# An expert stage in which the second layer of each pair of experts is issued one pair behind its first layer

## The reference, cut to what matters

```python
def body(acc, blk):
    tok, wt, e = blk
    xb = h[tok]
    hid = jax.nn.silu(xb @ w1[e]) * (xb @ w3[e])
    return acc.at[tok].add(wt[:, None] * (hid @ w2[e]).astype(f32)), None
...
routed, _ = lax.scan(body, jnp.zeros(h.shape, f32), (row_tok, row_w, block_e))
shared = (jax.nn.silu(h @ sw1) * (h @ sw3)) @ sw2
return routed.astype(h.dtype) + shared
```

## Time and profile before

| | |
|---|---|
| median of 3 runs | 2049.9 us (2045.67 to 2057.2) |
| the profiled execution: its own time | 2056.09 us |
| its span in the trace | 2054.3 us |
| mean granted PE clock | 0.951 |
| first first layer of the expert stage begins (pair 0) | 1387.0 us |
| last second layer of it begins (pair 47) | 2018.7 us |

### The profile page before, as it was taken

How to read it: one execution, slowest core, us unless ns; L and a number is a source line. 1 busy time by engine, 2 the same in 40 slices (tenths; PEclk the granted TensorE clock), 3 DMA queues, 4 the chain that set the end, 5 groups by cost and what they waited for, 6 DMA issues and landing times.

```text
span 2054.3 us, 33761 instructions
## 1 busy us (share of the span) xinstructions
PE 1905.8 (93%) x14498; PEld 1387.8 (68%) x14498; DVE 973.7 (47%) x1357; ACT 651.8 (32%) x1012; POOL 238.1 (12%) x226
## 2 busy tenths in 40 slices
PE   7979998999997999899998889979899999999993
PEld 7878998999987999665756779864344444444440
DVE  5745555556564777645555664762221111111116
ACT  5544334444454333320134523231111111111110
POOL 2100000000000000012100134301111111111213
PEclk9999999999998999999898799989999999999996
DMA  8535555544444876455410000187989989989886
GB/s 274 186 107 163 186 185 185 166 133 155 144 138 145 290 247 227 144 166 171 148 41 24 12 3 4 31 324 312 387 341 376 383 343 380 381 343 379 317 353 251
DMA packets 192326, 438.68 MB, mean 214 GB/s; under 512 B 24257, under 2 KB 145601, under 8 KB 163009
## 3 DMA queue, kind: packets, MB, share of 16 engines
q1 hardware_dynamic: 156336, 352.02, 46.7%
q0 software_dynamic: 23040, 43.05, 6.2%
q10 hardware_dynamic: 12816, 41.69, 5.3%
HBM read 501.68 MB, written 26.21 MB: 257 GB/s over the span
## 4 chain that ended last, share of the span: by engine, by line
PE 85%; DVE 8%; ACT 3%; DMA 3%; issue 1%; POOL 0%; SPq 0%; ACTq 0%; DVEq 0%; POOLq 0%
PE psum L344 32%; PE psum L3371 15%; PE psum L3392 8%; PE psum L1565 7%; PE psum L3342 4%; PE psum L1572 2%; PE psum L2602 2%; DMA mem<-in_exp_w_dram 1%; ACT w_hi L400 1%; PE psum L2586 1%; DVE mem L3496 1%; DVE w_lo L405 1%; PE psum L564 1%; PE psum L3132 1%; PE psum L1087 1%
## 5 line engine op out<-in xcount | busy, mean ns | idle before, releaser
L405 DVE TENSOR_TENSOR w_lo<-mem,w_hi 128x2048 fp32r<-128x2048 f32 x122 | 279.2, 2290 | 231.0 <-ACT w_hi L400 228.4
L344 PE MATMUL psum<-x_hi,w_hi 128*128 128x256 f32 x1216 | 349.7, 288 | 4.4 <-DVE x_lo L551 4.4
L3371 PE MATMUL psum<-mem 128*64 128x512 f32 x1536 | 342.7, 599 | 9.1 <-DMA mem<-in_exp_w_dram 9.1
L344 PE MATMUL psum<-x_hi,w_lo 128*128 128x256 f32 x1216 | 344.6, 283 | 0.0
L344 PE MATMUL psum<-x_lo,w_hi 128*128 128x256 f32 x1216 | 343.7, 283 | 0.0
L400 ACT ACTIVATE w_hi<-mem 128x2048 fp32r<-128x2048 f32 x122 | 233.8, 1918 | 193.8 <-PE psum L344 190.8
L3371 PEld LDWEIGHTS psum<-mem 128*64 128x64 f32 x1536 | 110.7, 138 | 233.1 <-issue 214.7
L344 PEld LDWEIGHTS psum<-x_hi,w_hi 128*128 128x128 f32 x1216 | 234.0, 192 | 10.1 <-DVE w_lo L405 4.7
L344 PEld LDWEIGHTS psum<-x_lo,w_hi 128*128 128x128 f32 x1216 | 237.5, 195 | 0.6
L344 PEld LDWEIGHTS psum<-x_hi,w_lo 128*128 128x128 f32 x1216 | 236.5, 194 | 0.0
L3392 PE MATMUL psum<-mem 128*64 128x512 f32 x768 | 177.2, 604 | 1.0 <-DVE mem L3443 1.0
(11 more groups left out here) (500 smaller groups left out, 2959.3 us busy)
## 6 DMA issues: line engine op xcount, KB each, us to landing
mem<-in_exp_w_dram SPq DMA_DIRECT2D x192, 1024.0 KB, 12.4
mem<-in_dil_w_qkv_dram SPq DMA_DIRECT2D x36, 1024.0 KB, 5.3
mem<-in_ada_w_dram POOLq DMA_DIRECT2D x48, 512.0 KB, 4.8
y_rows<-mem ACTq DMA_DIRECT2D x48, 512.0 KB, 7.9
mem<-in_ffn_w_gate_dram SPq DMA_DIRECT2D x22, 1024.0 KB, 5.6
mem<-in_ffn_w_up_dram SPq DMA_DIRECT2D x22, 1024.0 KB, 5.6
mem<-in_ffn_w_down_dram SPq DMA_DIRECT2D x22, 1024.0 KB, 4.7
mem<-in_w_in_dram SPq DMA_DIRECT2D x13, 1024.0 KB, 5.7
```

The costliest lines, as they stand in the source:

```text
L344: ins = pe.matmul(out, lhs[a], rhs[b], start=start and k == 0, stop=stop and k == 2, **kw)
L405: dve.tensor_tensor(w_lo[n % SLOTS][:, 0, :], ring[:, n % SLOTS, :], w_hi_f[n % HI][:, 0, :], ALU.subtract).then_inc(S("w_split"), 1)
L3371: ins = pe.matmul(psum[r, up, :].rearrange("p (a n) -> p a n", a=2), xg[:, b % 2, c, x * P + 64 * e:x * P + 64 * e + 64], w_up[s][e][:, :, ...
```

## The change

The second layer of pair k - 1 moves behind the first layer and the first gather call of pair k (the new function `down`), ahead of the transposes of pair k. DVE's scaling of a result (`y_dve`) and ACT's store follow it by one pair. SP issues the second-layer loads of pair k - 1 behind the first-layer loads of pair k, and POOL does so for spare pairs. The four additions of round 0 move behind the last pair. Nothing is computed in another way.

```diff
@@ moe_sp
-        for k, (kind, n) in enumerate(PAIRS):
-            if kind != "own":
-                continue
+        for k, (kind, n) in enumerate(PAIRS + [("end", 0)]):
...
-            if k >= 2:
-                sp.wait_ge(*at("mx_up", k - 1))
-            up_rows(k, n, range(2))
-            if k >= 2:
-                sp.wait_ge(*at("mx_y", k - 1))
-            down_rows(k, n, range(2))
+            if kind == "own":
+                if k >= 2:
+                    sp.wait_ge(*at("mx_up", k - 1))
+                up_rows(k, n, range(2))
+            if k == 0:
+                down_rows(k, n, range(2))
+            elif k >= 3 and PAIRS[k - 1][0] == "own":
+                sp.wait_ge(*at("mx_y", k - 2))
+                down_rows(k - 1, PAIRS[k - 1][1], range(2))
@@ moe_pool
+            if kind == "spare":
+                fetch_up(k, n)
+            if k > 2 and PAIRS[k - 1][0] == "spare":
+                fetch_down(k - 1, PAIRS[k - 1][1])
@@ moe_pe
+        def down(k):
+            s = k % 2
+            pe.wait_ge(*at("hid_T", k + 1))
+            pe.wait_ge(*loaded(k, "down_in", 32))
+            after(pe, "y1", k)
+            for h in range(2):
+                for f in range(2):
+                    for e in range(2):
+                        r = slice(64 * e, 64 * e + 64)
+                        ins = pe.matmul(psum[r, 4 + h, :], hid_T[:, f, r], w_down[s][e][:, f, 512 * h:512 * h + 512],
+                                        start=f == 0, stop=f == 1)
+            ins.then_inc(S("mx_y"), 1)
...
             if b + 1 < BATCHES:
                 gather_pe(pe, b + 1, 2 * x)
+            if k:
+                down(k - 1)
             pe.wait_ge(*at("mx_hid", k + 1))
...
             if b + 1 < BATCHES:
                 gather_pe(pe, b + 1, 2 * x + 1)
-            pe.wait_ge(*at("hid_T", k + 1))
...
-            ins.then_inc(S("mx_y"), 1)
+        down(len(PAIRS) - 1)
@@ moe_act
-            y_out(act, k)
+            if k:
+                y_out(act, k - 1)
+        y_out(act, len(PAIRS) - 1)
@@ moe_dve
             dve.tensor_tensor(hid_tok, sil, bank((0, 6)[k % 2], 256, 256), ALU.mult).then_inc(S("mx_hid"), 1)
+            if k:
+                y_dve(dve, k - 1)
             dve.wait_ge(*at("hid_turned", k + 1))
             after(dve, "mx_y", k)
             dve.tensor_copy(hid_T, bank(1, 256).rearrange("p (c j) -> p c j", c=2)).then_inc(S("hid_T"), 1)
-            if k == 47:
-                add_taken(dve, 0, 1)
-            dve.wait_ge(*at("mx_y", k + 1))
...
-            if k == 46:
-                add_taken(dve, 0, 0)
...
-        for r in range(1, 3):
+        y_dve(dve, len(PAIRS) - 1)
+        for r in range(3):
             for t in range(NT):
                 add_taken(dve, r, t)
```

More of the change, by code:

```diff
@@ L3310, in fetch, with fetch_up @@
                                     bounds_check=EXPERTS * P - 1, oob_is_err=False).then_inc(S(done), 16)
[L3312 to L3316, removed]
+        def fetch_up(k, n):
             pool.wait_ge(*at("mx_up", k - 1))
@@ L3319, in moe_pool, with fetch_down @@
                 for m, w in enumerate(("exp_w1_2", "exp_w3_2")):
-                    fetch(w_rows[s][2 * x + m], w, 2 * n + x, "spare_up_in")
+                    fetch(w_rows[k % 2][2 * x + m], w, 2 * n + x, "spare_up_in")
+        def fetch_down(k, n):
             pool.wait_ge(*at("mx_y", k - 1))
             for x in range(2):
-                fetch(w_rows[s][4 + x], "exp_w2_2", 2 * n + x, "spare_down_in")
+                fetch(w_rows[k % 2][4 + x], "exp_w2_2", 2 * n + x, "spare_down_in")
+        pool.wait_ge(*at("spare_rows", 3))
+        for k, (kind, n) in enumerate(PAIRS):
+            if kind == "spare":
+                fetch_up(k, n)
+            if k > 2 and PAIRS[k - 1][0] == "spare":
+                fetch_down(k - 1, PAIRS[k - 1][1])
     def after(eng, name, n):
@@ L3431, in one_hot_dve, with y_dve @@
                           ).then_inc(S("one_hot"), 1)
+    def y_dve(dve, k):
+        dve.wait_ge(*at("mx_y", k + 1))
+        if k >= 2:
+            dve.wait_ge(*at(f"y_out{k % 2}", 16 * (k // 2)))
+        dve.tensor_tensor(y[:, k % 2, :], banks(4, 2), g2_b, ALU.mult).then_inc(S("y1"), 1)
     def moe_dve(dve):
@@ L3443, in moe_dve @@
             dve.tensor_copy(hid_T, bank(1, 256).rearrange("p (c j) -> p c j", c=2)).then_inc(S("hid_T"), 1)
-            if k == 47:
-                add_taken(dve, 0, 1)
-            dve.wait_ge(*at("mx_y", k + 1))
-            if k >= 2:
-                dve.wait_ge(*at(f"y_out{k % 2}", 16 * (k // 2)))
-            dve.tensor_tensor(y[:, k % 2, :], banks(4, 2), g2_b, ALU.mult).then_inc(S("y1"), 1)
-            if k == 46:
-                add_taken(dve, 0, 0)
             if x and b + 2 < BATCHES:
```

## The result

| | before | after |
|---|---|---|
| median | 2053.55 us of 4 runs (2045.67 to 2064.53) | 2088.7 us of 4 runs (2082.22 to 2092.09) |
| ratio | | 1.016, 95% interval 1.0124 to 1.0196: 1.6% slower |
| profiled execution, span | 2056.09 us, 2054.3 us | 2085.75 us, 2083.9 us |
| expert stage: pair 0's first layer to the end of the span | 667.3 us | 705.2 us |
| of it pair 0 to pair 6 | 91.5 us | 87.7 us |

The account below looks back on a forecast made before the run. PE was taken as the bound in the middle of the expert stage. Terms -10.8 + 26.9 + 10.6 - 2.7 = +24.0 us on the median of 2049.9 gave 2074 us, range 2056 to 2091, chance 0.72.

Parts of the forecast that it names:

- start: Start of the expert stage: later second-layer loads cut load waits and the slow first layer; -10.8 us, bounds -12.3 to -7.4.
- new wait: Middle: an even pair's first layer waits for ACT's scaling of the gather right ahead; 23 x 1.17 = +26.9 us.
- crossings: Middle: PE changes between 128 and 64 columns of weights twice as often; 0.23 us a pair, +10.6 us.
- end: From pair 46 on: 8.0 us gained, 5.3 lost to round 0's additions; -2.7 us, bounds -2.7 to +2.7.
- The no-change rival: Middle: the wait for the scaling is not met, only shape changes are paid; -2.9 us, 2047 us, chance 0.09.
- pair 4, late by 6.96 us, is late by about 1.5 us: Start: pair 4's first layer still waits about 1.5 us for loads, taken as left over of 12.3 us.
- the load order gives nothing: Start, slower: pair 4 is as late as before; +34.8 us, 2085 us, chance 0.1.
- the term for late rows: End: fetched rows of round 0 may land up to 3.6 us late; counted only in the bounds.
- Costs at nothing: DVE's later copy, the transposes' wait, SP's and POOL's order, and stores a pair later: all hidden, no cost.
- The loads pace the middle: Middle, faster: loads set a pair's 12.90 us, so the added scaling wait costs nothing; -13.5 us, 2036 us, chance 0.05.
- Each gap lowers the clock: Middle, much slower: each of 23 gaps costs 3.19 us by a lower clock; adds 73 us, 2147 us, chance 0.04.

Follow-up runs that it names:

- the repeat: The unaltered changed kernel measured once more: 2092.0 us, before 2056.22, ratio 1.0175.
- the two kernels without spare loads: Kernel before and kernel after, each with fetches of spare experts' weights moving nothing: 2042.62 us (ratio 0.9941) and 2086.41 us (ratio 1.0163).
- first experiment: Changed kernel with the second gather call moved directly behind the first, ahead of the second layer: 2067.07 us, before 2051.91, ratio 1.0068.
- the spread kernel: Kernel before with spare places n and n + 16 in a spare pair instead of 2n and 2n + 1: 2049.53 us, ratio 0.9961.
- two crossings more: Kernel with both gather calls ahead of the second layer, altered to set the second call between that layer's halves: 2074.22 us, ratio 1.0093.
- loads as before: Changed kernel with second-layer loads and fetches issued in the order of the kernel before: 2186.06 us, before 2051.91, ratio 1.0643.
- no crossings more: Changed kernel with the lagging second layer behind transposes and both gather calls, two buffers for transposed rows: 2055.58 us, before 2051.91, ratio 1.001.

## Why the prediction was right, and where it was short

| term | predicted | measured | from |
|---|---|---|---|
| start | -10.8 | -5.2 (-7.2 in the repeat) | the two kernels without spare loads: 7.3 (5.3) left of 12.5 |
| new wait | +26.9 | +27.8 | 23 x 1.21, first experiment |
| crossings | +10.6 | +13.4 | 46 x 0.29, first and second |
| end | -2.7 | +3.0 | pair 46 to the end: 67.8 - 61.3, less 3.5 for the second layer of pair 45, which lies in that stretch only after |
| sum | +24.0 | +39.0 | stage: 705.2 - 667.3 = +37.9 |

The direction and the deciding term were right, but all four terms came out higher than forecast, and two of them, start and end, outside their own bounds. The total stayed inside the range because the wait and the crossings did not use up theirs. (The upper bounds add up to +43.5 us, not to the +41 of the range; the +35.2 lie inside either.)

**The new wait** was read rightly in place and size: 1.16 us idle against 1.17, 1.21 with the restart, once a batch. The no-change rival falls with it.

**The crossings** exist; the term was short by a quarter, inside its bounds (0 to 16). Taking two away and adding two gave 0.29 and 0.33 us for two; the rows of before, added up, gave 0.23. The Trainium skill's rule ("TensorEngine Tiling (Array Packing)", Key Properties: a change of tiling mode drains TensorE) agrees with the traces in that more changes of shape cost more time; it gives no price, the two runs do.

**The start** is the step that failed: "pair 4, late by 6.96 us, is late by about 1.5 us". The term measured -5.2 us, and -7.2 in the repeat, where its bounds were -12.3 and -7.4. For pair 4 alone the number came nearly true, in part by luck: its first layer starts 55.8 us behind pair 0's, where 54.8 was forecast (1441.8 - 1387.0), but it does not wait for loads at all. It is 2.9 us later than in the kernel after without spare loads (52.95 us) because pair 2 ahead of it was late. The lateness went to other pairs. Without pair 0's second layer ahead, pair 2 is due 24.3 us behind pair 0 in place of 27.4, and its fetches are not there; pair 5's fetches are asked for at 1428 to 1432, and the last needs 18.36 us, as the chain of waits after shows:

```profile
1431.99 18.36 DMA mem<-in_exp_w_dram,mem
```

From pair 2's first layer to pair 5's the loads move 420 GB/s, nearly the 424 of the earlier trace rows:

```profile
1405.33:1450.40 45.07, 41.29 (x199) 17.41 (x199) 12.08 (x35) 7.26 (x15) 5.93 (x6) 0.96 1.01 420
```

So at the start the transfer rate is the limit, and an order decides mainly who waits, as the load order alone showed. Taking bytes away (both kernels without spare loads) or to later (the spread kernel) removes most of the waits; the change removed 5.2 and 7.2 of 12.5 us. The rival "the load order gives nothing" was nearer in its total (+34.8) than the forecast, for a cause that was about half right.

**The end.** The last scaling came as forecast (26.77 us against 26.7). What failed is the term for late rows, taken as nothing. The bounds allowed up to 3.6 us for the rows of round 0 and 1.8 us for a slow clock in the last second layer. Neither came so: that layer takes 3.65 us, the rows of round 0 cost 1.57 us, and those of round 1, which the forecast did not count, another 3.85. These waits are paid in full. In the five profiled executions in which the second layer stands ahead of the transposes and no loads are late at the end (after, its repeat, without spare loads, first experiment, two crossings more) they are 5.42, 5.21, 5.61, 6.69 and 6.13 us, and the stretch from pair 46 to the end less these waits is 62.33 to 62.35 us each time: 62.34 - 61.28 - 3.5 = -2.4, close to the -2.7 forecast. Moving the additions alone cost nothing that could be measured (+0.04%). Why the rows are late is read from the timeline and was not tried by itself: the store of pair 45 took 8.81 us to POOL's next step, about the upper of the two values named, and POOL fetches round 1 behind round 0.

**Costs at nothing** held in the change: nothing waits for the later copy but the last second layer (1.22 us, within the hand-overs that the end counted), and SP has no late element. The two load experiments show how much that rests on: the change without its load order costs 134 us, the load order without the rest 88, both together 35.

**The other rivals.** *The loads pace the middle*: no. PE idles, the period grows by the wait and the crossings in full, and the loads move less, 347 GB/s. *Each gap lowers the clock*: no. The granted clock is 1.00 over 100 us with three such gaps (100 - 96.53 = 3 x 1.16). The Trainium skill's rule for it ("TensorE: Matmul & The Clock Gate", section on psum-queue depth-cycling), by which frequent short idling makes the clock go back and forth, does not show in this trace: gaps of 1.16 us every 27.5 us left the clock at 1.00, its upper level of 2.4 GHz.

What stays open: the sum of the measured terms is 1.1 us above what the stage shows, which one execution of each kernel cannot settle, and why pair 2 waits in one execution of the kernel after and pair 3 in another.

## What to carry to other kernels

Before a piece of work is moved away from between a producer and its consumer, ask what it was covering there: here 3.58 us of second layer hid 1.2 us of scaling, once a batch, and the move cost 28 us without adding any work. The order in which loads are issued and the order in which they are used are one decision: here either without the other cost 2.5 to 4 times as much as both together. Where the transfer rate itself is the limit, as at the start of this stage, move bytes to a place where the rate has room (0.4% faster here, with three spare experts to load) rather than reorder them.

## What the runs showed of the hardware that was not expected

- The length of an idle gap alone did not tell what clock the first layer behind it got. Gaps of up to 2.13 us left the granted clock at 1.00 (7.09 us), and so did one of 2.31 us (all four additions between the last copy and the last scaling) and one of 3.52 us (loads as before). Gaps of 2.28, 2.62 and 2.67 us (after and its repeat), another of 2.31 us (loads as before) and two of 2.75 and 2.83 us (no crossings more) were followed by first layers of 8.78 us at a clock of 0.81, and all gaps from 3.97 to 7.58 us by 8.41 to 10.06 us at 0.70 to 0.84.
- Two changes of PE between 128 and 64 columns of weights cost about 0.3 us, in two comparisons of kernels (0.29 and 0.33), while the listed time of a first layer only goes from 7.04 to 7.09 us.
- POOL's fetches of spare weights took up to 19.7 us to land before and 18.4 after, while SP's loads were in flight (after, the median of all is 4.1 us); SP's four first-layer loads, issued behind two others, took 20.8 us in the kernel with the loads as before.
